# A weight unit's high-part products ahead of its low-part products; norms, transposes and products by halves of 512 columns

## The chip, the cores and the metric

The kernel runs on one core of one Trainium2 chip. The metric is the device time of one execution in microseconds. TensorE is called PE here, VectorE is DVE, ScalarE is ACT, GpSimd is POOL, and SyncE, which issues the large loads, is SP.

## What is computed

One sequence of 256 tokens with 1024 features goes through two blocks, all in float32. The first block has two hybrid layers (a linear-recurrent mixer beside banded attention, then a squared-ReLU network of width 4096). The second has a pooling mixer with a gated network of width 2816, then a sparse-attention mixer and eight gated experts of width 3584, of which every token uses two. Cut to the parts that the change touches:

```python
def hybrid_layer(x, ...):                      # twice
    h = rms_norm(x, norm1_g)
    proj = h @ w_in
    ...
    x = x + jnp.concatenate([y_m, y_a], axis=-1) @ w_out
    u = jax.nn.relu(rms_norm(x, norm2_g) @ w_up)
    return x + (u * u) @ w_down

def second_block(x, ...):
    for i in range(DEPTH):                     # i = 0: pool and swiglu, i = 1: nsa and experts
        ...
        x = layer_norm(ALPHA * x + h, ln_g[i, 0], ln_b[i, 0])
        ...
        x = layer_norm(ALPHA * x + f, ln_g[i, 1], ln_b[i, 1])

def swiglu(x, w_gu, w_down):
    g, u = jnp.split(x @ w_gu, 2, axis=-1)
    return (jax.nn.silu(g) * u) @ w_down
```

## The kernel before

**Units.** All weights are laid out ahead of time as 491 units of up to 128 x 2048 numbers (1 MB). SP loads them in order into a ring of four slots, and of six in the experts (`slot`, `sync_program`); a slot is loaded anew once DVE has read it (`low.of(last)`). For each unit ACT rounds the weights to a shorter float format and writes `HI` (`split_hi`, L499), and then DVE writes the rest, weight minus `HI`, as `LO` (`split_lo`, L507). `HI` and `LO` have three buffers each, and ACT waits until PE has used unit u - 3 (`used`).

**Products.** Activations are split in the same way into `XTH` and `XTL` (of the rows, turned) or `HTH` and `HTL` (of a network's hidden values). A product is taken as high x high, high x low weight, and low activation x high weight, three matmuls for each block of 128 rows (`group3`, L517). An expert with up to 64 tokens is packed: its high and low activations stand side by side in 128 columns, and two matmuls do (`group2`, L527). PE takes all matmuls of a block of rows before it goes to the next block, so the second matmul of a unit already needs `LO`; it waits for `low.of(u)` ahead of the whole unit, in `col_part` (units by columns: projections, and "up" and "gate" of a network), in `row_part` ("down") and in `few` (units of 8 to 48 columns).

**Norms.** Two tiles of 128 tokens (t = 0 and 1) follow one another. `rms_apply` and `ln_apply` end with one DVE instruction over all 1024 columns (L740, L775) into `ROWS` or `X`. `turn_rows` waits for it (`rows_at`), turns the first four blocks of 128 columns into one bank (L693) and the other four into the next. ACT copies each bank to `XTH` (`cols_hi`, L701) and DVE writes the rest to `XTL` (`cols_lo`, L709). The products wait for the second bank (`x_ready`, the event "cols", t, 4). The functions put matmuls without use, on constants, where PE would stand still (`idle`, L675, and `idle_first`, L682).

**A network.** `net_tensor` goes over chunks c of 512 hidden columns: two units up, two units gate (where it is gated), then the turning of chunk c - 1 (`net_turn_tensor`, L1032; for a packed expert matmuls against `pairs`, L1027), then two units down of chunk c - 2. ACT and DVE take the units in the same order, two units ahead of PE. On ACT, `net_turn_scalar` for a packed expert holds in this order: the silu of the turned bank (L1042), one unit of `split_hi`, the copy to the high half of `HTH` (L1058), and the other units. On DVE, `net_turn_vector` holds the product with the gate (L1068), one unit of `split_lo`, the low half (L1084), and the other units. Each engine works strictly in its own order. In the execution shown, expert 0 has one full and one packed tile, experts 1 to 3 one full tile each, and experts 4 to 7, from about 1825 us on, one packed tile each.

Of the kernel before, what the change touches and what calls it, by code (L numbers as in the profile page):

```python
# [16 lines left out]
P = 128  # L17
# [348 lines left out]
def build(nc, d, out, tables):  # L366
    at, cons_cols, units, place = tables
    dense = len(units) - N_EXP * d["experts"].shape[1]
    with ExitStack() as ctx:
# [143 lines left out]
        def group3(e, out_ap, trios, start, stop):  # L513
            n, m = 0, 3 * len(trios)
            for lh, ll, rh, rl in trios:
                for a, b in ((lh, rh), (lh, rl), (ll, rh)):
                    ins = e.matmul(out_ap, lhsT=a, rhs=b, start=start and n == 0,  # L517
                                   stop=stop and n == m - 1)
                    n += 1
            return ins  # L520

        def group2(e, out_ap, duos, start, stop):

            n, m = 0, 2 * len(duos)
            for both, rh, rl in duos:
                for b in (rh, rl):
                    ins = e.matmul(out_ap, lhsT=both, rhs=b, start=start and n == 0,  # L527
                                   stop=stop and n == m - 1)
                    n += 1
            return ins  # L530
# [6 lines left out]
        def col_part(e, use, t, u, i, last, kinds, a, x_ready):  # L537
# [4 lines left out]
            for w in x_ready(t):  # L542
                e.wait_ge(*w)
            e.wait_ge(*low.of(u))
            if kinds[t] == P:
                xh, xl = (XTH, XTL) if u < dense else (XM[:, 0], XM[:, 1])
                ins = group3(e, bank[:, 0:n], [
                    (xh[:, i * kk + k, a:a + P], xl[:, i * kk + k, a:a + P], hv[:, k, :], lv[:, k, :])
                    for k in range(kk)], i == 0, last)
            else:  # L550
                ins = group2(e, bank[:, 0:n], [
                    (XP[:, i * kk + k, 2 * a:2 * a + P], hv[:, k, :], lv[:, k, :])
                    for k in range(kk)], i == 0, last)
# [34 lines left out]
        def row_part(e, use, t, u, i, kb, hb, first, stop, kinds, h_ready):  # L588

            hv, lv = hi_lo(u)  # L590
            for w in h_ready:
                e.wait_ge(*w)
            e.wait_ge(*low.of(u))
            for nh in range(2):
                end = stop and 2 * i + 2 == kb
                if kinds[t] == P:
                    ins = group3(e, banks.get(*use, t, nh), [
                        (HTH[:, hb, 2 * i + k, tile(t)], HTL[:, hb, 2 * i + k, tile(t)],
# [33 lines left out]
        def x_ready(name):  # L632

            return lambda t: [v_bank.of(name, "cols", t, 4)]

        def few(e, use, key, x_ready):
# [5 lines left out]
            for t in range(2):  # L642
                for w in x_ready(t):
                    e.wait_ge(*w)
# [2171 lines left out]
```

## Time and profile before

| | |
|---|---|
| Median of three runs | 2314.14 us (2311.27 to 2316.27) |
| The profiled execution | 2311.63 us |
| Its span | 2309.8 us |
| Busy in the span | PE 2154.1 us, DVE 1595.7, ACT 1322.8 |
| Granted TensorE clock, mean | 0.977 |
| HBM read | 521.48 MB, 226 GB/s over the span |

The span is the time from the first to the last instruction; 1.8 us of the execution lie around it. The chain of waits is read from the last instruction back: at each step to what released it. A bracket behind a row of the timeline gives how long the engine had been idle and what ended that. PE's matmuls overlap, and a busy time counts each to its modelled end (0.39 us for 512 columns), so the pace of a stream is read from the distance between starts. The share of the DMA engines passes 1.00 by a little where they are full, since their packets overlap.

### The profile page before, as it was taken

What the parts mean: (1) busy time and instruction counts of PE and PEld (TensorE: products, weight loads), DVE (VectorE), ACT (ScalarE), POOL (GpSimd) and SP (SyncE); (2) the same over time, 40 slices, a digit from 0 to 9 for tenths busy, and PEclk for the clock granted to TensorE, in tenths of its full rate; (3) what the DMA queues carried; (4) which work ended last, traced back from release to release, by engine and by line L of the source; (5) the groups of instructions that cost most, each with busy time, mean ns of one, the idle gap of its engine ahead of it and who ended that gap; (6) DMA issues with size and microseconds to landing.
All of it is one profiled execution on the core that took longest, in us unless ns stands there. A gap on an engine that the chain in (4) does not pass through costs nothing.

```text
span 2309.8 us, 26107 instructions
## 1 busy us (share of the span) xinstructions
PE 2154.1 (93%) x10090; PEld 1723.0 (75%) x10090; DVE 1595.7 (69%) x1538; ACT 1322.8 (57%) x1376; POOL 22.1 (1%) x33
## 2 busy tenths in 40 slices
PE   8889999989999999998888999999999989898987
PEld 6667887767788788776667888788888776666665
DVE  4965555776555644565745554888888889898997
ACT  5554444644444444436534544676767778787886
POOL 0000000000000000000000000000000000000000
PEclk9989999999999999997899999999999999999999
DMA  6314553431655355441007555698888999999995
GB/s 259 137 46 150 182 182 129 165 119 69 243 186 186 137 183 195 150 148 59 1 19 281 199 214 194 255 373 344 346 346 338 373 348 415 350 411 352 411 369 216
DMA packets 74337, 524.29 MB, mean 227 GB/s; under 512 B 8704, under 2 KB 9152, under 8 KB 11872
## 3 DMA queue, kind: packets, MB, share of 16 engines
q1 hardware_dynamic: 71424, 511.64, 58.4%
q0 software_dynamic: 2784, 10.93, 1.3%
q8 instruction: 82, 1.34, 0.2%
q14 instruction: 47, 0.39, 0.0%
HBM read 521.48 MB, written 1.05 MB: 226 GB/s over the span
## 4 chain that ended last, share of the span: by engine, by line
PE 71%; DVE 16%; ACT 8%; issue 5%; DMA 0%; DVEq 0%; ACTq 0%; POOLq 0%
PE psum L517 51%; PE psum L527 8%; DVE LO L507 6%; ACT HI L499 3%; PE psum L1027 3%; DVE AR L1512 1%; PE psum L2362 1%; PE psum L1032 1%; PE psum L2390 1%; PE psum L881 1%; ACT AR L847 1%; DVE XT L709 1%; PE psum L693 1%; PE psum L675 1%; PE psum L818 1%
## 5 line engine op out<-in xcount | busy, mean ns | idle before, releaser
L507 DVE TENSOR_TENSOR LO<-ring,HI 128x2048 fp32r<-128x2048 f32 x379 | 851.4, 2259 | 415.4 <-ACT HI L499 409.2
L499 ACT ACTIVATE HI<-ring 128x2048 fp32r<-128x2048 f32 x379 | 713.0, 1886 | 339.9 <-PE psum L517 279.5
L517 PE MATMUL psum<-HI,XT 128*128 128x512 f32 (+1 forms) x2592 | 827.6, 394 | 34.9 <-DVE XT L709 12.1
L517 PEld LDWEIGHTS psum<-HI,XT 128*128 128x128 f32 x2592 | 493.7, 191 | 159.1 <-DVE XT L709 24.5
L517 PE MATMUL psum<-LO,XT 128*128 128x512 f32 (+1 forms) x1296 | 506.7, 391 | 0.0
L507 DVE TENSOR_TENSOR LO<-AR,HI 128x2048 fp32r<-128x2048 f32 x112 | 254.3, 2290 | 48.3 <-ACT HI L499 47.8
L517 PEld LDWEIGHTS psum<-LO,XT 128*128 128x128 f32 x1296 | 248.0, 191 | 48.5
L527 PE MATMUL psum<-HI,XT 128*128 128x512 f32 x560 | 231.1, 413 | 39.9 <-DVE LO L507 38.4
L499 ACT ACTIVATE HI<-AR 128x2048 fp32r<-128x2048 f32 x112 | 213.4, 1911 | 61.5 <-PE psum L527 37.4
L517 PE MATMUL psum<-HI,HTH 128*128 128x512 f32 x568 | 225.1, 396 | 0.0
L517 PE MATMUL psum<-HI,HTL 128*128 128x512 f32 x568 | 221.6, 390 | 0.0
L517 PE MATMUL psum<-LO,HTH 128*128 128x512 f32 x568 | 221.2, 389 | 0.0
L527 PE MATMUL psum<-LO,XT 128*128 128x512 f32 x560 | 220.4, 394 | 0.0
L527 PEld LDWEIGHTS psum<-HI,XT 128*128 128x128 f32 x560 | 105.5, 188 | 99.2 <-issue 40.7
L990 ACT ACTIVATE AR<-psum 128x512 f32<-128x512 f32 (+1 forms) x107 | 63.5, 594 | 111.1 <-PE psum L517 92.0
L517 PEld LDWEIGHTS psum<-HI,HTL 128*128 128x128 f32 x568 | 106.6, 188 | 22.7
L517 PEld LDWEIGHTS psum<-LO,HTH 128*128 128x128 f32 x568 | 106.8, 188 | 21.1
L517 PEld LDWEIGHTS psum<-HI,HTH 128*128 128x128 f32 x568 | 106.7, 188 | 20.8
L527 PEld LDWEIGHTS psum<-LO,XT 128*128 128x128 f32 x560 | 105.8, 189 | 20.6 <-issue 1.0
L527 PE MATMUL psum<-HI,HTH 128*128 128x512 f32 x280 | 112.6, 402 | 5.0 <-DVE HTH L1084 4.6
L527 PE MATMUL psum<-LO,HTH 128*128 128x512 f32 x280 | 109.5, 391 | 0.0
L1048 ACT ACTIVATE HTH<-psum 128x512 fp32r<-128x512 f32 (+1 forms) x72 | 42.7, 593 | 57.4 <-PE psum L1032 52.8
(279 smaller groups left out, 1886.7 us busy)
## 6 DMA issues: line engine op xcount, KB each, us to landing
ring<-in_experts SPq DMA_DIRECT2D x224, 1024.0 KB, 6.8
ring<-in_dense SPq DMA_DIRECT2D x149, 1024.0 KB, 4.8
AR<-in_experts SPq DMA_DIRECT2D x112, 1024.0 KB, 6.7
bcs<-in_ln_g POOLq DMA_DIRECT2D x4, 512.0 KB, 4.3
bcs<-in_ln_b POOLq DMA_DIRECT2D x4, 512.0 KB, 5.1
bcs<-in_norm_g POOLq DMA_DIRECT2D x3, 512.0 KB, 4.0
cons<-in_cons POOLq DMA_DIRECT2D x1, 1317.0 KB, 8.1
X<-in_x SPq DMA_DIRECT2D x2, 512.0 KB, 4.2
```

The source lines that it names most:

```text
L499: e.activation(HI[:, h:h + m], slot(u), ACT.Copy).then_inc(*high.up(u))
L507: e.tensor_tensor(LO[:, h:h + m], slot(u), HI[:, h:h + m].bitcast(F32), ALU.subtract).then_inc(*low.up(u))
L517: ins = e.matmul(out_ap, lhsT=a, rhs=b, start=start and n == 0, stop=stop and n == m - 1)
L527: ins = e.matmul(out_ap, lhsT=both, rhs=b, start=start and n == 0, stop=stop and n == m - 1)
L675: e.matmul(bank, lhsT=ident, rhs=cons[:, 0:512], start=True, stop=True)
L693: ins = e.transpose(bank[:, j * P:(j + 1) * P], src(k0 + j), ident)
L709: e.tensor_tensor(XTL[:, k0:k0 + 4, tile(t)], banks.get(name, "cols", t, k0).rearrange("p (k s) -> p k s", k=4), XTH[:, k0:k0 + 4, tile(t) ...
L818: e.matmul(bank[:, 0:2 * nk], lhsT=a.qT[:, b, tile(qt)], rhs=a.kz(kind, b)[:, :, 0:nk], start=True, stop=True).then_inc(*filled.up(a.name, ...
L847: e.activation(w3[:, h, :], w3[:, h, :], ACT.Exp, bias=nm[:, h:h + 1], accum_out=l[:, 2 * b + h:2 * b + h + 1]).then_inc(*a_done.up(a.name ...
L990: e.activation(GS[:, hb, t, 0:n], banks.get(use, "up", c, t)[:, 0:n], f).then_inc(*a_bank.up(use, "up", c, t))
L1027: ins = e.matmul(bank[:, o:o + PACK], lhsT=src[:, tile(j)], rhs=C("pairs"), start=True, stop=True)
L1048: e.activation(HTH[:, hb, 0:nb, tile(t)], bank[:, 0:n].rearrange("p (j s) -> p j s", j=nb), ACT.Copy).then_inc(*a_done.up(use, "turn", c, t))
```

## The change

1. `products` takes the place of `group3` and `group2`. For a unit, PE waits for `high.of(u)` and does all matmuls on `HI` (8 in a full tile, 4 in a packed one); then it waits for `low.of(u)` and does those on `LO` (4). Their number is the same. In `row_part` the high-part matmuls of both halves stand ahead of the low-part ones of both.
2. `x_ready` takes the block that is needed: a unit of blocks 0 to 3 waits for the first turned bank alone.
3. `rms_apply` and `ln_apply` end with two instructions over 512 columns each, and `turn_rows` waits for each half by itself. Where the rows come from the mixers (`y_tile`), each half waits for its own event.
4. The output goes out in four DMAs of 512 columns in place of two of 1024.

```diff
+        def products(e, out_ap, pairs, start, stop):
+
+            for n, (a, b) in enumerate(pairs):
+                ins = e.matmul(out_ap, lhsT=a, rhs=b, start=start and n == 0,
+                               stop=stop and n == len(pairs) - 1)
             return ins
...
-            for w in x_ready(t):
+            for w in x_ready(t, kk * (i + 1) - 1):
                 e.wait_ge(*w)
+            if kinds[t] == P:
+                xh, xl = [z[:, i * kk:i * kk + kk, a:a + P] for z in
+                          ((XTH, XTL) if u < dense else (XM[:, 0], XM[:, 1]))]
+                first = [(z[:, k], hv[:, k, :]) for k in range(kk) for z in (xh, xl)]
+            else:
+                xh = XP[:, i * kk:i * kk + kk, 2 * a:2 * a + P]
+                first = [(xh[:, k], hv[:, k, :]) for k in range(kk)]
+            e.wait_ge(*high.of(u))
+            products(e, bank[:, 0:n], first, i == 0, False)
             e.wait_ge(*low.of(u))
...
+            ins = products(e, bank[:, 0:n], [(xh[:, k], lv[:, k, :]) for k in range(kk)], False, last)
...
+            e.wait_ge(*high.of(u))
+            for nh in range(2):
+                products(e, banks.get(*use, t, nh), [
+                    (z[:, hb, 2 * i + k, tile(t)], hv[:, k, half(nh)]) for k in range(2)
+                    for z in ((HTH, HTL) if kinds[t] == P else (HTH,))], first and i == 0, False)
             e.wait_ge(*low.of(u))
...
-            return lambda t: [v_bank.of(name, "cols", t, 4)]
+            return lambda t, k: [v_bank.of(name, "cols", t, k // 4 * 4)]
...
-                for w in ready:
+                for w in ready(k0 // 4):
                     e.wait_ge(*w)
...
-            e.scalar_tensor_tensor(dst[:, t, :], X[:, t, :], r, gv, ALU.mult,
-                                   ALU.mult).then_inc(*v_done.up(name, "rows", t))
+            for nh in range(2):
+                e.wait_ge(*g_at)
+                e.wait_ge(*v_order.last)
+                e.scalar_tensor_tensor(dst[:, t, half(nh)], X[:, t, half(nh)], r, gv[:, half(nh)],
+                                       ALU.mult, ALU.mult).then_inc(*v_done.up(name, "rows", t, nh))
+            v_done.mark(name, "rows", t)
...
             for t in range(2):
-                e.wait_ge(*v_done.of("l3", "rows", t))
-                e.dma_start(out[0, tile(t), :], X[:, t, :]).then_inc(s_out, 16)
-            e.wait_ge(s_out, 32)
+                for nh in range(2):
+                    e.wait_ge(*v_done.of("l3", "rows", t, nh))
+                    e.dma_start(out[0, tile(t), half(nh)], X[:, t, half(nh)]).then_inc(s_out, 16)
+            e.wait_ge(s_out, 64)
```

PE before, in a chunk of the last packed expert: the end of the second unit "gate", and the turning behind it (`HI` and `LO` are the weight's parts, `XT` the activations; a wait stands with the instruction that it holds up).

```order
L527 MATMUL psum<-HI,XT 128x512 [waits s_low]
L527 MATMUL psum<-LO,XT 128x512
L527 MATMUL psum<-HI,XT 128x512
L527 MATMUL psum<-LO,XT 128x512
L527 MATMUL psum<-HI,XT 128x512
L527 MATMUL psum<-LO,XT 128x512
L527 MATMUL psum<-HI,XT 128x512
L527 MATMUL psum<-LO,XT 128x512
L1027 MATMUL psum<-cons,AR 128x64 [waits s_a_bank]
L1027 MATMUL psum<-cons,AR 128x64 x7
```

PE now, in the same place:

```order
L516 MATMUL psum<-HI,XT 128x512 [waits s_high]
L516 MATMUL psum<-HI,XT 128x512 x3
L516 MATMUL psum<-LO,XT 128x512 [waits s_low]
L516 MATMUL psum<-LO,XT 128x512 x3
L1025 MATMUL psum<-cons,AR 128x64 [waits s_a_bank]
L1025 MATMUL psum<-cons,AR 128x64 x7
```

The wait for DVE has moved from ahead of eight matmuls to ahead of the last four, and one wait, for ACT, has come in ahead of the first.

DVE before, at the program's start: the norm of tile 0, its columns' low part, the norm of tile 1, and the low parts of the first two units.

```order
L740 SCALAR_TENSOR_TENSOR AR<-X,SML,bcs 128x1024 [waits s_v_done,s_first]
L709 TENSOR_TENSOR XT<-psum,XT 128x4x128 [waits s_v_done,s_a_done]
L709 TENSOR_TENSOR XT<-psum,XT 128x4x128 [waits s_v_bank,s_a_done]
L733 TENSOR_TENSOR SML<-SML 128x1 [waits s_v_bank,s_a_done]
L737 RECIPROCAL SML<-SML 128x1 [waits s_v_done,s_a_done]
L740 SCALAR_TENSOR_TENSOR AR<-X,SML,bcs 128x1024 [waits s_v_done]
L507 TENSOR_TENSOR LO<-ring,HI 128x2048 [waits s_high] x2
```

DVE now, in the same place:

```order
L731 SCALAR_TENSOR_TENSOR AR<-X,SML,bcs 128x512 [waits s_v_done,s_first]
L731 SCALAR_TENSOR_TENSOR AR<-X,SML,bcs 128x512 [waits s_v_done]
L699 TENSOR_TENSOR XT<-psum,XT 128x4x128 [waits s_v_done,s_a_done]
L699 TENSOR_TENSOR XT<-psum,XT 128x4x128 [waits s_v_bank,s_a_done]
L723 TENSOR_TENSOR SML<-SML 128x1 [waits s_v_bank,s_a_done]
L727 RECIPROCAL SML<-SML 128x1 [waits s_v_done,s_a_done]
L731 SCALAR_TENSOR_TENSOR AR<-X,SML,bcs 128x512 [waits s_v_done] x2
L507 TENSOR_TENSOR LO<-ring,HI 128x2048 [waits s_high] x2
```

Each norm's last instruction has become two of half its columns; nothing else on DVE has changed its place, and ACT's order is the same as before.

## Rows read from the trace of the kernel before

**Rows 1.** Chain of waits, whole program; start us, us, engine, line, instructions

```profile
by line: PE psum L517 51.4%; PE psum L527 8.3%; DVE LO L507 6.2%; issue 5.0%; ACT HI L499 3.3%; PE psum L1027 2.6%; DVE AR L1512 1.4%; PE psum L2362 1.3%; PE psum L1032 1.3%; PE psum L2390 1.0%; PE psum L881 0.9%; ACT AR L847 0.7%; DVE XT L
...
365.39 21.79 PE psum L517 x96
```

**Rows 2.** Who waited for whom, 1850 to 2250 us; us, times, longest

```profile
PE psum L527 <- DVE LO L507: 34.7, 53, 1.9
DVE LO L507 <- ACT HI L499: 30.9, 42, 1.4
```

**Rows 3.** Stretches; PE, PEld, DVE, ACT, POOL busy, clock, DMA share, GB/s

```profile
1650.00:1700.00 50.00, 50.00 (x227) 41.36 (x226) 44.14 (x25) 36.23 (x24) 0.00 (x0) 1.00 0.94 366
...
1904.40:1919.80 15.40, 13.86 (x66) 10.50 (x65) 14.06 (x8) 12.87 (x11) 0.00 (x0) 1.00 1.01 420
...
1850.00:2250.00 400.00, 360.16 (x1695) 273.62 (x1696) 356.97 (x225) 319.72 (x261) 0.00 (x0) 1.00 0.96 379
```

**Rows 4.** Timeline, one chunk of a packed expert; start us, us, engine, line

```profile
1893.77 4.49 DVE L507 TENSOR_TENSOR LO<-AR,HI 128x2048 fp32r<-128x2048 f32 x2
...
1898.31 0.50 PE L527 MATMUL psum<-HI,XT 128*128 128x512 f32 x1
...
1898.49 4.49 DVE L507 TENSOR_TENSOR LO<-ring,HI 128x2048 fp32r<-128x2048 f32 x2 [0.24 <-ACT HI L499]
...
1900.26 1.89 PE L1027 MATMUL psum<-cons,AR 128*128 128x64 f32 x16
...
1902.19 0.38 ACT L1042 ACTIVATE AR<-psum 128x256 f32<-128x256 f32 x1 [1.13 <-PE psum L1027]
...
1902.47 1.91 ACT L499 ACTIVATE HI<-ring 128x2048 fp32r<-128x2048 f32 x1
...
1902.90 0.41 DVE L1068 TENSOR_TENSOR AR<-AR,psum 128x256 f32<-128x256 f32 x1
...
1904.41 2.29 DVE L507 TENSOR_TENSOR LO<-ring,HI 128x2048 fp32r<-128x2048 f32 x1 [1.10 <-ACT HI L499]
...
1906.62 0.42 DVE L1084 TENSOR_TENSOR HTH<-AR,HTH 128x256 fp32r<-128x256 f32 x1
```

**Rows 5.** Timeline, second norm of layer 0

```profile
196.69 1.03 PE L693 MATMUL psum<-cons,AR 128*128 128x128 f32 x8
...
197.56 1.02 PE L675 MATMUL psum<-cons 128*128 128x512 f32 x2
197.96 1.49 DVE L709 TENSOR_TENSOR XT<-psum,XT 128x512 fp32r<-128x512 f32 x2 [2.93 <-ACT XT L701]
...
199.50 0.50 PE L517 MATMUL psum<-HI,XT 128*128 128x512 f32 x1 [0.91 <-DVE XT L709]
...
202.79 0.50 PE L517 MATMUL psum<-HI,XT 128*128 128x512 f32 x1 [0.27 <-DVE LO L507]
...
205.67 1.28 DVE L740 SCALAR_TENSOR_TENSOR AR<-X,SML,bcs 128x1024 f32<-128x1024 f32 x1
...
207.01 1.09 PE L693 MATMUL psum<-cons,AR 128*128 128x128 f32 x8 [0.35 <-DVE AR L740]
...
209.88 0.50 PE L517 MATMUL psum<-HI,XT 128*128 128x512 f32 x1 [0.91 <-DVE XT L709]
```

**Rows 6.** Timeline, the program's start

```profile
14.42 3.69 ACT L499 ACTIVATE HI<-ring 128x2048 fp32r<-128x2048 f32 x2
...
16.35 4.49 DVE L507 TENSOR_TENSOR LO<-ring,HI 128x2048 fp32r<-128x2048 f32 x2 [0.32 <-ACT HI L499]
...
18.79 0.47 PE L517 MATMUL psum<-HI,XT 128*128 128x512 f32 x1 [3.23 <-DVE LO L507]
...
24.32 1.03 PE L693 MATMUL psum<-cons,AR 128*128 128x128 f32 x8
```

**Rows 7.** Timeline, the norm ahead of the router

```profile
1199.31 1.97 PE L693 MATMUL psum<-cons,X 128*128 128x128 f32 x8 [3.21 <-DVE X L775]
...
1202.74 0.67 PE L517 MATMUL psum<-XT,HI 128*8 128x256 f32 x2
```

More of the change, by code:

```diff
@@ L595, in row_part @@
                 end = stop and 2 * i + 2 == kb
-                if kinds[t] == P:
-                    ins = group3(e, banks.get(*use, t, nh), [
-                        (HTH[:, hb, 2 * i + k, tile(t)], HTL[:, hb, 2 * i + k, tile(t)],
-                         hv[:, k, half(nh)], lv[:, k, half(nh)]) for k in range(2)],
-                        first and i == 0, end)
-                else:
-                    ins = group2(e, banks.get(*use, t, nh), [
-                        (HTH[:, hb, 2 * i + k, tile(t)], hv[:, k, half(nh)], lv[:, k, half(nh)])
-                        for k in range(2)],
-                        first and i == 0, end)
+                ins = products(e, banks.get(*use, t, nh), [
+                    (HTH[:, hb, 2 * i + k, tile(t)], lv[:, k, half(nh)]) for k in range(2)], False, end)
                 if (t, nh) == (len(kinds) - 1, 1):
@@ L642, in few @@
             for t in range(2):
-                for w in x_ready(t):
+                for w in x_ready(t, KB - 1):
                     e.wait_ge(*w)
+            e.wait_ge(*high.of(u))
+            products(e, bank[0:n, 0:S], [(hv[:, i, :], z[:, i, :]) for i in range(KB)
+                                         for z in (XTH, XTL)], True, False)
             e.wait_ge(*low.of(u))
-            ins = group3(e, bank[0:n, 0:S], [
-                (hv[:, i, :], lv[:, i, :], XTH[:, i, :], XTL[:, i, :]) for i in range(KB)], True, True)
+            ins = products(e, bank[0:n, 0:S], [(lv[:, i, :], XTH[:, i, :]) for i in range(KB)],
+                           False, True)
             ins.then_inc(*used.up(u))
@@ L1317, in second_rows @@
             def second_rows():
-                turn_rows(e, n1, 1, lambda k: ROWS[:, 1, tile(k)], rows_at(n1, 1), wait=l, rest=l, b=BA[0])
+                turn_rows(e, n1, 1, lambda k: ROWS[:, 1, tile(k)], rows_of(n1, 1), wait=l, rest=l, b=BA[0])
                 if l == 0:
@@ L1773, in pool_tensor @@
             idle(e, 3)
-            turn_rows(e, "l0", 0, lambda k: X[:, 0, tile(k)], [v_done.of("l0", "rows", 0)], rest=0)
+            turn_rows(e, "l0", 0, lambda k: X[:, 0, tile(k)], rows_of("l0", 0), rest=0)
             mixed_tensor(e, 1)
@@ L1950, in sparse_tensor @@
             xr = x_ready("l1")
-            turn_rows(e, "l1", 0, lambda k: X[:, 0, tile(k)], [v_done.of("l1", "rows", 0)])
+            turn_rows(e, "l1", 0, lambda k: X[:, 0, tile(k)], rows_of("l1", 0))
             cols_by_tile(e, ("q0", 2), ("q0", 2), BOTH, xr, between=lambda: turn_rows(
-                e, "l1", 1, lambda k: X[:, 1, tile(k)], [v_done.of("l1", "rows", 1)], wait=1, b=BA[0]))
+                e, "l1", 1, lambda k: X[:, 1, tile(k)], rows_of("l1", 1), wait=1, b=BA[0]))
             cols(e, ("q1", 2), ("q1", 2), BOTH, xr)
@@ L2419, in experts_tensor @@
         def experts_tensor(e):
-            turn_rows(e, "l2", 0, lambda k: X[:, 0, tile(k)], [v_done.of("l2", "rows", 0)])
-            turn_rows(e, "l2", 1, lambda k: X[:, 1, tile(k)], [v_done.of("l2", "rows", 1)], wait=4)
+            turn_rows(e, "l2", 0, lambda k: X[:, 0, tile(k)], rows_of("l2", 0))
+            turn_rows(e, "l2", 1, lambda k: X[:, 1, tile(k)], rows_of("l2", 1), wait=4)
             few(e, ("gates", 3), ("gates", 3), x_ready("l2"))
```

58 lines of the change are left out of this document (17 added, 41 removed).

## Prediction

> **What bounds the kernel now.** I read the chain of waits first. 51% of it is matmuls at L517, the full tiles; 8% is L527, the packed tiles; 6% is DVE's `LO` and 3% ACT's `HI`. A run of 96 matmuls over four units takes 21.79 us, 0.227 us each, with no pause at any unit's start [rows 1]. There PE is the bound, and an order that adds and removes no matmul gives nothing. In 1650 to 1700 us, experts with a full tile, PE is busy for all 50 us [rows 3].
>
> So the gain has to come from two other kinds of place. One is experts 4 to 7, the last 470 us. In 1850 to 2250 us PE waits 34.7 us for `LO`, 53 times, and DVE waits 30.9 us for `HI`, 42 times [rows 2]. DVE is busy 357.0 of these 400 us, and the DMA engines are at a share of 0.96 [rows 3]: three resources stand near their limit. The other kind is the norms, where PE stands still while DVE, PE, ACT and DVE hand one tile on [rows 5 to 7].
>
> **Packed experts: the cycle.** Rows 4 is one chunk, and the pattern comes back every 15.40 us: the `LO` of "down" at 1898.49 is that of the next chunk at 1913.9. The reader is to follow it round. DVE ends the `LO` of the second gate unit at 1893.77 + 4.49 = 1898.26. PE starts that unit's 8 matmuls at 1898.31 and turns at 1900.26: 1.95 us. Turning takes until 1902.15, the silu starts at 1902.19, and only behind it, at 1902.47, does ACT take the `HI` of the next chunk's first unit. DVE gets it for its `LO` at 1904.41, after 1.10 us of idling. Then come four `LO`, 2.2 us apart, and the small L1084 (1906.62, a step of 0.34), and the ring closes at 1913.66. The two `LO` of "down" (1898.49, 4.49 us) run beside PE's and ACT's part.
>
> Now the four matmuls on `HI` can run before 1898.26, since that `HI` was ready before DVE read it. Four of eight remain behind `LO`: 1.95 - 4 x 0.23 = 1.03 us. Turning, silu, `HI` and the next `LO` come 0.92 us earlier, and the cycle becomes 15.40 - 0.92 = 14.48 us. DVE is next: it is busy 14.06 of 15.40 us in a chunk [rows 3], so 1.34 us of idling (1.10 and 0.24) are there, and 0.92 fits. PE has slack: 48 x 0.23 + 1.89 = 12.9 us. From 1825 us to the end there are some 28 such cycles with those that hold an expert's change: 28 x 0.92 = 26 us, and 0.9 at the very end, where four matmuls run ahead of the last `LO`. That is 27 us if nothing else stands in the way.
>
> **Packed experts: the loads.** A chunk reads six units, 6 x 1.049 = 6.29 MB. In the chunk of 1904.4 to 1919.8 us the DMA share is 1.01 at 420 GB/s [rows 3]. At that pace six units take 6.29 / 0.420 = 15.0 us, more than the 14.48 that the cycle asks for. Over the 400 us the share is 0.96 at 379 GB/s: there are stretches at a full share and a lower rate, so not every packet moves at the best pace, and I take the share and not the best rate as the measure. What DMA could still give is 1 - 0.96 / 1.01 = 5%, 20 us in 400. It can't all be had: at an expert's change DVE does other work, the six slots are full and the queue pauses, whatever the pace elsewhere. I take four fifths, 16 us, in place of 27. Ends for the range: 27 (loads never bind), and 2 (loads give nothing, but four matmuls at the very end and slack in the ring remain). 16 is nearer to the row of 0.96.
>
> The Trainium skill (DMA: Bandwidth & Descriptors, "Where 436 GB/s comes from") says that for loads from HBM the HBM side binds at about 358 GB/s, and names 435 GB/s as the ceiling of the ports. By the first, an estimate, a chunk would take 6.29 / 0.358 = 17.6 us, which the trace contradicts with 15.40 [rows 3, 4]. By the second it would take 14.46 us, the loads would not bind, and the sum would be the 27 us of the second rival; the row with a share of 1.01 at 420 speaks against it.
>
> **Start** [rows 6]. PE waits 3.23 us for the first `LO` (ended 18.65). The `HI` of that unit ends at 16.3. Its 8 matmuls then run to 18.2, the 4 others from 18.7 to 19.6, and the second unit (8 matmuls, then 4, its `LO` ready by 20.8) to 22.4. Tile 1 is turned then and not at 24.32: 1.9 us. Behind it PE needs only the first turned bank, 0.8 us earlier (below). Together 2.7 us.
>
> **Norms, tile 0** [rows 5]. PE turns at 196.69, fills with a useless matmul until 198.6, and waits for both banks of L709 (197.96 + 1.49 = 199.45). With the first bank alone (half of the 1.49) it goes on at 198.7: 0.8 us. At 202.79 it waits for the `LO` of the second unit, 0.27 us and a slow restart; this goes too. But the gain of tile 0 is not kept by itself: tile 1's norm stands behind that `LO` on DVE, which doesn't move.
>
> **Norms, tile 1** [rows 5]. The norm's last step runs 205.67 to 206.95, and PE, which by then waits, turns at 207.01. Two instructions over 512 columns take 1.49 us at L709, about 0.75 each, where the one over 1024 takes 1.28. So the first half is there at 206.4, and the second at 207.16, 0.2 us later than before. PE turns four blocks, then four more, fills until 208.5, and goes on at 208.55 in place of 209.88. So 1.3 us for the norm. The 0.2 us are paid on DVE at each norm, and they are hidden behind PE's first four blocks; where nobody uses the halves (the norm ahead of pooling), they show.
>
> The same pattern stands at three norms of the hybrid layers (3 x 1.3 = 4.0), at the one after pooling (1.1, less the 0.2 of the norm ahead of it) and ahead of the sparse layer (1.8, since there tile 0's norm is late as well). At the two mixer outputs both tiles gain (2 x 1.4), at the sparse one tile 1 alone (0.8). Ahead of the router the second half of the turning runs at the lower clock, and both tiles' norms are on the path: 1.3 of the 3.4 us from 1199.31 to 1202.74 [rows 7]. The first expert and the output give 0.7. Sum: 2.7 + 4.0 + 1.1 + 1.8 + 2.8 + 0.8 + 1.3 + 0.7 = 15.2 us. What follows each place (mixers, DVE's chains) is moved as a whole; the loads of the dense units are far ahead there. Bounds: 9 (only tile 1's half turns up) to 19.
>
> **Sum.** 15 + 16 = 31 us off the profiled 2311.6: 2280.6. The median of the runs lies 2.5 above the profiled one, so 2283.
>
> **Rivals.** *Loads don't bind.* The packed experts run at 14.48 us per chunk: 15 + 27 = 42 us off, 2272. For it: no wait for a landing in any view. Against: a share of 1.01.
>
> *Loads give nothing more.* The stretches of low rate at a full share are how the engines behave when asked for more; then only the norms and the end stay: 15 + 2 = 17 off, 2297. For it: 1.01 in a chunk of 15.40 us. Against: 0.96 in the mean.
>
> *Slower: each new wait costs a restart.* PE gets one more wait in each of 491 units. Where a wait really holds PE up, the next matmul starts late: the step from the first to the second is 0.34 us and not 0.23 (from 24 matmuls in 5.53 us at the start, 18.79 to 24.32 [rows 6], one sees 0.23). If an unneeded wait in the middle of a group cost the same 0.11 us, 491 x 0.11 = 54 us would stand against 31: 2314 + 23 = 2337. It turns to slower from 31 / 491 = 0.063 us for a wait. Against it: the 96 matmuls of rows 1 pass four such satisfied waits at 0.227 us each; 0.063 us would be seen.
>
> *It doesn't do what it says* would be PE still waiting for `LO` as long as before; then some 5 us from the norms' halves, within what can't be told apart.
>
> **Chances.** Loads bind in part, 2283: 0.58. Loads don't bind, 2272: 0.16. Loads give nothing more, 2297: 0.19. Within 0.2% (about what a measurement of this kernel can tell from no change): 0.03. Slower: 0.04. So faster 0.93. The range goes from the bound of the second case, with 19 for the norms (2314 - 46 = 2268), to that of the third with 11 to 13 (2300).
>
> **What would show it.** In the profile after: PE's wait for `LO` at the start at most 0.5 us; PE's start of the second unit's matmuls at 22.4 us less the tile's turn; the three norms' resumption 1.3 us earlier against their turn. In the packed experts a chunk of 14.8 to 15.0 us, a DMA share of 1.00 or more in all stretches from 1850 us on, and, new, ACT's `HI` waiting for landings; the wait of DVE for `HI` in other chunks below 0.3 us. A chunk of 14.5 us is the first rival, one of 15.3 the second. In full tiles 0.227 us for a matmul; anything above shows the slower rival. Wrong would be the whole sum if PE, with its matmuls earlier, met the bank evictions of ACT as a new wait at each chunk.

## The result and the profile after

The changed kernel takes 2275.97 us in the median (2274.03 to 2279.28). The ratio to the kernel before is 0.984, with an interval of 0.9823 to 0.9857. The profiled execution takes 2274.03 us where that of before took 2311.63: 37.6 us less. Forecast were 31 us less and a median of 2283 us, in a range of 2268 to 2300. Sign and size came out; the way there partly did not.

The waits in 1850 to 2250 us, for [rows 2]. The columns are us in total, times, longest.

```profile
PE psum L516 <- DVE LO L507: 12.4, 21, 2.0
...
DVE LO L507 <- ACT HI L499: 17.6, 26, 1.4
...
ACT HI L499 <- DMA AR<-in_experts: 1.5, 3, 0.6
...
ACT HI L499 <- DMA ring<-in_experts: 0.6, 2, 0.4
```

Each of the first two was over 30 us. The last two are new and small: ScalarE waits for a landing, five times. All products now stand at L516.

The stretches, for [rows 3] (busy of PE, PEld, DVE, ACT, POOL; clock, DMA share, GB/s):

```profile
1650.00:1700.00 50.00, 50.00 (x224) 41.24 (x223) 43.21 (x24) 37.05 (x25) 0.00 (x0) 1.00 0.98 372
1850.00:2250.00 400.00, 375.29 (x1773) 285.89 (x1772) 373.98 (x237) 334.70 (x274) 0.00 (x0) 1.00 0.97 396
1889.00:1904.40 15.40, 14.36 (x67) 10.80 (x67) 14.88 (x10) 13.63 (x11) 0.00 (x0) 1.00 1.01 419
```

PE and DVE are 15 and 17 us busier in the same 400 us, and the loads bring 396 GB/s in place of 379. One chunk, for [rows 4]:

```profile
1880.51 1.89 PE L1025 MATMUL psum<-cons,AR 128*128 128x64 f32 x16
...
1882.44 0.39 ACT L1040 ACTIVATE AR<-psum 128x256 f32<-128x256 f32 x1 [1.13 <-PE psum L1025]
1882.72 1.91 ACT L499 ACTIVATE HI<-ring 128x2048 fp32r<-128x2048 f32 x1
...
1884.67 2.29 DVE L507 TENSOR_TENSOR LO<-ring,HI 128x2048 fp32r<-128x2048 f32 x1 [0.51 <-ACT HI L499]
...
1893.82 4.49 DVE L507 TENSOR_TENSOR LO<-ring,HI 128x2048 fp32r<-128x2048 f32 x2
...
1895.01 1.89 PE L1025 MATMUL psum<-cons,AR 128*128 128x64 f32 x16
...
1896.94 0.39 ACT L1040 ACTIVATE AR<-psum 128x256 f32<-128x256 f32 x1 [1.13 <-PE psum L1025]
```

Turning starts at 1880.51 and again at 1895.01, the silu at 1882.44 and 1896.94: a chunk is 14.50 us and was 15.40. (The four middle steps of the first three packed experts are 14.47 to 14.53 us, and were 15.39 to 15.45; most are 14.48.) DVE idles 0.51 us for the `HI` behind the silu, not 1.10, and the idling of 0.24 ahead of the two `LO` of "down" is gone. That is the ring of the prediction, shorter by 0.92 us to within what one reads.

Where the 37.6 us went I read from the ends of `LO` of the same weight units in both traces. Up to the 330th unit (about 1850 us) the changed kernel is 16.7 us ahead. From there to the last unit it takes 419.7 us and not 440.1, 20.4 less. The 330th is the seventh unit of expert 4; from that expert's first unit to it both traces take 18.5 us, so all that the packed experts gain lies behind it. The tail gives 0.4.

### The profile page after: what moved, and what is told of

It reads as the page before. It is cut to its first block, busy times and chain, and to the rows that moved or that the text cites. A ratio compares the mean times of both kernels' runs of the same rounds, so it can differ in the third digit from the quotient of the medians.

```text
span 2272.2 us, 26134 instructions
## 1 busy us (share of the span) xinstructions
PE 2151.1 (95%) x10090; PEld 1724.3 (76%) x10090; DVE 1597.7 (70%) x1556; ACT 1320.2 (58%) x1376; POOL 22.1 (1%) x33
## 3 DMA queue, kind: packets, MB, share of 16 engines
q8 instruction: 82, 1.34, 0.2%
## 4 chain that ended last, share of the span: by engine, by line
PE 70%; DVE 18%; ACT 6%; issue 5%; DMA 0%; DVEq 0%; ACTq 0%; SPq 0%; POOLq 0%
PE psum L516 58%; DVE LO L507 10%; ACT HI L499 3%; PE psum L1025 2%; DVE AR L1508 1%; PE psum L1030 1%; PE psum L2358 1%; PE psum L816 1%; PE psum L879 1%; PE psum L1895 1%; PE psum L664 1%; PE psum L683 1%; ACT AR L845 1%; PE psum L2386 1%; PE psum L1272 1%
## 5 line engine op out<-in xcount | busy, mean ns | idle before, releaser
L516 PE MATMUL psum<-HI,XT 128*128 128x512 f32 (+1 forms) x3152 | 805.1, 394 | 21.0 <-issue 5.8
L516 PEld LDWEIGHTS psum<-HI,XT 128*128 128x128 f32 x3152 | 592.2, 191 | 164.0 <-issue 13.1
L516 PE MATMUL psum<-LO,XT 128*128 128x512 f32 (+1 forms) x1856 | 507.5, 395 | 18.6 <-DVE LO L507 14.4
L516 PEld LDWEIGHTS psum<-LO,XT 128*128 128x128 f32 x1856 | 342.7, 190 | 123.0 <-DVE LO L507 56.6
L516 PE MATMUL psum<-HI,HTH 128*128 128x512 f32 x848 | 303.3, 398 | 4.9 <-DVE HTH L1082 4.9
L516 PE MATMUL psum<-LO,HTH 128*128 128x512 f32 x848 | 227.2, 390 | 0.0
L516 PE MATMUL psum<-HI,HTL 128*128 128x512 f32 x568 | 221.5, 390 | 0.0
L516 PEld LDWEIGHTS psum<-HI,HTH 128*128 128x128 f32 x848 | 157.3, 188 | 37.0 <-DVE HTH L1082 6.5
L516 PEld LDWEIGHTS psum<-LO,HTH 128*128 128x128 f32 x848 | 159.2, 188 | 33.9
L516 PEld LDWEIGHTS psum<-HI,HTL 128*128 128x128 f32 x568 | 106.8, 188 | 21.0
L845 ACT ACTIVATE AR<-AR,SML 128x256 f32<-128x256 f32 (+1 forms) x96 | 45.4, 473 | 44.7 <-DVE SML L837 40.8
L1025 PEld LDWEIGHTS psum<-cons,AR 128*128 128x128 f32 x560 | 66.8, 192 | 3.0 <-ACT AR L996 1.2
L1025 PE MATMUL psum<-cons,AR 128*128 128x64 f32 x560 | 66.6, 272 | 1.0 <-ACT AR L996 1.0
L1072 DVE TENSOR_TENSOR HTL<-psum,HTH 128x512 fp32r<-128x512 f32 (+1 forms) x72 | 49.3, 684 | 22.5 <-ACT HTH L1046 16.9
L816 PE MATMUL psum<-AR 128*128 128x512 f32 (+1 forms) x96 | 54.0, 656 | 11.2 <-DVE AR L833 7.0
L691 ACT ACTIVATE XT<-psum 128x512 fp32r<-128x512 f32 x40 | 23.9, 597 | 64.4 <-PE psum L683 63.4
```

The lines of the kernel that those rows point to most:

```text
L691: e.activation(XTH[:, k0:k0 + 4, tile(t)], banks.get(name, "cols", t, k0).rearrange("p (k s) -> p k s", k=4), ACT.Copy).then_inc(*a_done.u ...
L816: e.matmul(bank[:, 0:2 * nk], lhsT=a.qT[:, b, tile(qt)], rhs=a.kz(kind, b)[:, :, 0:nk], start=True, stop=True).then_inc(*filled.up(a.name, ...
L845: e.activation(w3[:, h, :], w3[:, h, :], ACT.Exp, bias=nm[:, h:h + 1], accum_out=l[:, 2 * b + h:2 * b + h + 1]).then_inc(*a_done.up(a.name ...
L1025: ins = e.matmul(bank[:, o:o + PACK], lhsT=src[:, tile(j)], rhs=C("pairs"), start=True, stop=True)
L1072: e.tensor_tensor(HTL[:, hb, 0:nb, tile(t)], bank[:, 0:n].rearrange("p (j s) -> p j s", j=nb), xh.bitcast(F32), ALU.subtract).then_inc(*v_ ...
```

## The experiments

Two columns recur below. "Ahead" is the time to the end of `LO` of the 330th unit, "packed" that from there to the last unit's.

| kernel | median us | ratio to before (95%) | ahead | packed |
|---|---|---|---|---|
| before | 2312.4 to 2314.1 | 1 | 1849.9 | 440.1 |
| after | 2276.0 | 0.984 (0.9823 to 0.9857) | 1833.2 | 419.7 |
| products_only | 2289.2 | 0.9889 (0.9864 to 0.9913) | 1852.3 | 419.9 |
| halves_only | 2300.6 | 0.9942 (0.9924 to 0.9959) | 1839.2 | 439.8 |
| one_unit | 2307.3 | 0.9974 (0.9961 to 0.9988) | 1846.2 | 434.0 |
| two_units | 2296.0 | 0.9927 (0.9910 to 0.9943) | 1850.5 | 423.3 |
| more_waits | 2276.5 | 0.9847 (0.9831 to 0.9864) | 1835.1 | 419.9 |
| light_loads | 2277.5 | 0.985 (0.9834 to 0.9867) | 1838.0 | 419.6 |
| hi_early | 2271.4 | 0.9831 (0.9808 to 0.9853) | 1832.3 | 416.1 |
| hi_early_light | 2262.3 | 0.9786 (0.9770 to 0.9803) | 1833.7 | 407.6 |
| fill | 2275.1 | 0.9827 (0.9804 to 0.985) | 1837.6 | 420.9 |
| after_again | 2274.8 | 0.984 (0.9822 to 0.9857) | 1833.5 | 419.8 |

### Each part alone

products_only takes the halves out of the changed kernel: the norms' last step, the waits ahead of turning, the waits for turned columns and the output transfer are whole again.

```diff
-            for nh in range(2):
-                e.scalar_tensor_tensor(dst[:, t, half(nh)], X[:, t, half(nh)], r, gv[:, half(nh)], ...
+            e.scalar_tensor_tensor(dst[:, t, :], X[:, t, :], r, gv, ALU.mult, ...
...
-            return lambda t, k: [v_bank.of(name, "cols", t, k // 4 * 4)]
+            return lambda t, k: [v_bank.of(name, "cols", t, 4)]
```

> The changed kernel with its norms, transposes, waits for turned columns and output transfer whole again (1024 columns), so that only the order of the products is new. Theory (the two parts are independent and add up): the chunk of the packed experts stays at 14.48 us, 20.4 us are gained from 1815 us on, 2 at the start (the first LO wait) and 1 in small restarts: 2288 us, a ratio of 0.990 to the kernel before, that is 13 us above the changed kernel. Rival (the halves are needed for the order to pay, or the other way round): under 5 us between this kernel and the changed one.

halves_only keeps these and restores the old order of products. Here is `col_part`, the branch taken alone; `row_part` and `few` are changed in the same way:

```diff
-            e.wait_ge(*high.of(u))
-            products(e, bank[:, 0:n], first, i == 0, False)
             e.wait_ge(*low.of(u))
-            ins = products(e, bank[:, 0:n], [(xh[:, k], lv[:, k, :]) for k in range(kk)], False, last)
+            ins = products(e, bank[:, 0:n], [
+                q for k in range(kk) for q in ([first[m * k], second[k]] + first[m * k + 1:m * k + m])],
+                i == 0, last)
```

> The changed kernel with the products in the order of the kernel before (high, low, high of each block, one wait for LO), norms, transposes and waits by halves kept. Theory (parts add up): the chunk is back at 15.40 us, the three norms of the hybrid layers keep 1.3 us each, in sum 13 to 14 us from the norms and transposes: 2298 us, ratio 0.994. Rival (part of the 16.7 us before the packed experts is not from the halves but from where TensorE's granted clock happens to fall): the sum comes out between 8 and 20 us, and the difference from 14 stands in stretches in which the clock is at 1.2 GHz in one kernel and at 2.4 in the other.

The packed experts get all of their gain from the order (419.9 against 419.7) and none from the halves (439.8 against 440.1). Ahead of them it is the other way round. A stretch in which the clock stays at 2.4 GHz in all of them shows it best: from the 21st to the 56th unit, the whole first feed-forward with a norm at either end. First before, then after:

```profile
202.74:410.91 208.17, 202.95 (x921) 164.80 (x922) 112.47 (x96) 92.77 (x90) 0.54 (x1) 1.00 0.47 168
```

```profile
194.14:399.65 205.51, 201.31 (x917) 163.74 (x916) 113.23 (x99) 92.77 (x90) 0.54 (x1) 1.00 0.48 171
```

Then halves_only and products_only:

```profile
200.56:406.22 205.66, 202.60 (x921) 164.85 (x922) 113.12 (x99) 92.77 (x90) 0.54 (x1) 1.00 0.48 171
```

```profile
199.33:407.49 208.16, 202.12 (x921) 164.44 (x920) 112.56 (x97) 92.74 (x90) 0.54 (x1) 1.00 0.48 168
```

2.7 us for two norms with both parts, 2.5 with the halves alone, 0.0 with the order alone. The sum of the parts' medians, 23.2 and 11.8 us, is 35.0, within a few us of the whole (36.9): the parts add up as closely as these medians can tell.

### Which wait closes the ring

one_unit is the kernel before with the new order in one of a chunk's six units, two_units in both gate units:

```diff
+            if kinds[t] == PACK and len(kinds) == 1 and use[1] == "gate" and last:
+                e.wait_ge(*high.of(u))
+                products(e, bank[:, 0:n], first, i == 0, False)
+                e.wait_ge(*low.of(u))
+                ins = products(e, bank[:, 0:n], second, False, last)
```

(two_units leaves out `and last`.)

> The kernel before (order, norms and transposes), with the new order of products in a single place: the second gate unit of each chunk in the experts whose only tile is packed. Theory (the ring of waits runs through that unit alone): the chunk is 14.48 us as in the changed kernel, the gain is the 20 us of the packed experts, 2291 us, ratio 0.991. Rival (each unit's wait for LO takes part): one of six units changed gives about a sixth, 3 to 4 us, 2308 us, chunk 15.3.

My theory fell here. The ring does pass through this unit, as the prediction followed it, but a chunk takes 15.09 us and 6.1 us are gained in all, not 20. (A spell of low clock from 1972.4 us, of 3.4 us, hides some 1.6 more: the expert that it falls in takes 115.2 us, the one before it 113.6. It doesn't save the theory.) The timeline of PE in one_unit:

```profile
1891.53 0.47 PE L516 MATMUL psum<-HI,XT 128*128 128x512 f32 x1 [0.18 <-DVE LO L507]
...
1893.45 1.07 PE L516 MATMUL psum<-HI,XT 128*128 128x512 f32 x4
1894.35 1.08 PE L516 MATMUL psum<-LO,XT 128*128 128x512 f32 x4
1895.27 1.89 PE L1035 MATMUL psum<-cons,AR 128*128 128x64 f32 x16
...
1910.36 1.89 PE L1035 MATMUL psum<-cons,AR 128*128 128x64 f32 x16
```

PE starts the first gate unit behind its `LO`, at 1891.53, and then has 16 matmuls in a row. It gets to the second unit's four on `HI` at 1893.45 only, and to the four on `LO` at 1894.35, although DVE wrote that `LO` by 1893.6. The bound has moved one unit back: from the end of the first gate unit's `LO` to turning it takes 1895.27 - 1891.39 = 3.88 us, and took 1900.26 - 1896.06 = 4.20 [rows 4]. That is the 0.31 us of the chunk.

> The kernel before, with the new order of products in both gate units of each chunk in the experts whose only tile is packed. With the second gate unit alone the chunk was 15.08 us, not 14.48: TensorE, which ran all 8 matmuls of the first gate unit behind that unit's LO, had 16 matmuls in a row (16 x 0.23 = 3.7 us) from there, and they ended 0.33 us earlier than before and no more. Theory: with both gate units changed, four matmuls of each are ahead of their LO, TensorE waits for the second LO again, and the chunk is 14.48 us: the gain is the 20 us of the packed experts, 2291 us, ratio 0.991. Rival (the up and down units count as well): the chunk comes out between 14.6 and 15.0 us, 2296 to 2303 us.

16.8 of the 20.4 us. The chunk:

```profile
1916.97 2.29 DVE L507 TENSOR_TENSOR LO<-ring,HI 128x2048 fp32r<-128x2048 f32 x1 [0.33 <-ACT HI L499]
...
1931.63 2.29 DVE L507 TENSOR_TENSOR LO<-ring,HI 128x2048 fp32r<-128x2048 f32 x1 [0.34 <-ACT HI L499]
```

14.66 us, 0.18 above the 14.48 of most chunks of the full change. The four other units of a chunk bring that rest; that it is the up units, which still run all behind their `LO` and so push PE a little late into the gate units, is my reading, and no run takes them by themselves. So of the 0.92 us the last gate unit alone brings 0.31, the unit ahead of it 0.43, the rest 0.18. Here a wait at the end of a run of units was left behind only as far as PE had caught up before it.

### The price of a wait

```diff
             for n, (a, b) in enumerate(pairs):
+                if probe:
+                    e.e.wait_ge(*probe)
                 ins = e.matmul(out_ap, lhsT=a, rhs=b, ...
```

> The changed kernel with a wait (always satisfied: the same HI that the unit's first matmul waited for) ahead of each of the 8 matmuls on HI of the up and gate units with a full tile in the experts, some 780 waits more. Theory (a satisfied wait costs nothing): 2276 us, 0.227 us for a matmul. Rival (each costs the restart of 0.11 us): 86 us more, 2362 us; the point at which the whole change would have turned slower, 0.063 us, would show as 49 us more, 2325 us.

From the 198th to the 330th unit (the experts with one full tile, and the first units of the next) it is 409.4 us with the added waits and 409.2 without. PE in 1600 to 1650 us, where each matmul on `HI` of an up or gate unit has its wait:

```profile
1600.00:1650.00 50.00, 50.00 (x240) 42.05 (x239) 42.38 (x26) 34.92 (x24) 0.00 (x0) 1.00 0.88 341
```

240 matmuls start there, and 238 in the changed kernel. The slower rival is out: at the 0.063 us where it would have decided, 49 us would be missing.

### Do the loads bind?

light_loads halves every load from the fifth expert on; the other half of each slot keeps old weights, so the products there are of old numbers while the engines' work stays the same. hi_early has full loads and a quicker ring: ScalarE's `HI` goes ahead of the silu, so that DVE needn't wait for it. hi_early_light has both.

```diff
+                dst = slot(u)
+                if u >= dense and x >= 4:
+                    dst, src = dst[:, 0:UNIT // 2], src[:, 0:UNIT // 2]
-                e.dma_start(slot(u), src).then_inc(s_ring[i], 16)
+                e.dma_start(dst, src).then_inc(s_ring[i], 16)
```

```diff
+            alone = tuple(kinds) == (PACK,)
+            if alone:
+                between()
             for t, kind in enumerate(kinds):
...
-            between()
+            if not alone:
+                between()
```

> The changed kernel, with each load of the packed experts (from the fifth expert on) fetching half of its unit, so that the products there use old weights in the other half; the engines' work is the same in number and size. Theory (the loads are at the edge in the changed kernel but hold it up for only some 2 us, as its waits of ScalarE for landings show): 2270 to 2274 us, chunk still 14.48 us. Rival (the loads are what is left of the bound there): the packed experts speed up by 8 us or more, to 2267 us or less, with a chunk below 14.4.

> The changed kernel, with ScalarE's HI of the next chunk's first unit in front of the silu and not behind it, in the experts whose only tile is packed. Theory (VectorE's wait for this HI, 0.51 us in a chunk, is the last slack of the ring, and the loads still have some: 42 units landing every 2.49 us are 104.6 us of an expert's 110.3): the chunk is 13.97 us, 22 x 0.5 = 11 us less than the changed kernel, 2265 us, ratio 0.980; ScalarE's waits for landings grow by some us. Rival (the loads bind at 14.5 us already): the chunk stays at 14.4 to 14.5, 2274 to 2278 us, and what VectorE no longer waits for HI, ScalarE waits for landings, some 10 us more.

> The kernel with ScalarE's HI ahead of the silu, with half-size loads as in the other one. Theory (with full loads it stayed at 2271 because six landings of 2.49 us are 14.94 us, more than its 13.97): without that bound the chunk is 13.97 us, 22 x 0.5 = 11 us less than with half loads alone, 2260 to 2262 us. Rival (VectorE or TensorE bounds it at the same time, not the loads): within 3 us of the other kernel with half loads.

In the changed kernel the loads cost nothing that can be read: half the bytes, DMA share 0.60 in place of 0.97, and the packed experts take 419.6 us in place of 419.7.

```profile
1850.00:2250.00 400.00, 376.45 (x1784) 286.24 (x1782) 374.22 (x237) 333.13 (x272) 0.00 (x0) 1.00 0.60 200
```

(The median of light_loads is 1.5 us above that of the changed kernel; its trace is 4.8 us later at the 330th unit, and all but the last few loads up to there are whole. More on that below.)

With the quicker ring they do. hi_early gains 3.6 us in the packed experts where the ring allows 12.1 (407.6 with half loads, my 11 and a little). Who waits for landings in hi_early, 1850 to 2250 us, and one piece of ScalarE:

```profile
ACT HI L499 <- DMA ring<-in_experts: 8.3, 14, 1.6
...
ACT HI L499 <- DMA AR<-in_experts: 4.5, 9, 0.6
```

```profile
1900.98 1.92 ACT L499 ACTIVATE HI<-AR 128x2048 fp32r<-128x2048 f32 x1 [0.58 <-DMA AR<-in_experts]
...
1903.47 1.92 ACT L499 ACTIVATE HI<-ring 128x2048 fp32r<-128x2048 f32 x1
1905.96 1.91 ACT L499 ACTIVATE HI<-ring 128x2048 fp32r<-128x2048 f32 x1 [0.57 <-DMA ring<-in_experts]
...
1908.45 1.92 ACT L499 ACTIVATE HI<-ring 128x2048 fp32r<-128x2048 f32 x1
```

From 1900.98 on a `HI` starts each 2.49 us, 0.02 us behind its landing, and six landings there (1900.95 to 1915.89) are 14.94 us. PE follows some units behind. Within the expert it still turns every 13.88 us; the time is lost where the next expert begins:

```profile
1892.49 1.89 PE L1025 MATMUL psum<-cons,AR 128*128 128x64 f32 x16
...
1906.36 1.89 PE L1025 MATMUL psum<-cons,AR 128*128 128x64 f32 x16
1911.83 1.89 PE L1025 MATMUL psum<-cons,AR 128*128 128x64 f32 x16
...
1945.90 1.90 PE L1025 MATMUL psum<-cons,AR 128*128 128x64 f32 x16
```

The last step is 34.07 us; in hi_early_light it is 31.25 (1913.15 to 1944.40). At the next two changes of expert 1.9 and 2.1 us are lost in the same way, 6.8 of the 8.5 us in all. So the chunk of my theory came, 13.88 us for 13.97, and the gain didn't; the rival's chunk of 14.4 to 14.5 didn't come, and its waits for landings did (8.3 + 4.5 us). I had set the landings against the mean of an expert alone, 104.6 us against 110.3; even the 107.2 that an expert takes in hi_early_light leave room for them, and still the loads bind. hi_early is the quickest kernel with whole loads, but its interval (0.9808 to 0.9853) overlaps that of the changed kernel, so I don't call it better.

### TensorE's clock ahead of the packed experts

The order changes nothing at the norms, and yet products_only is 2.4 us *later* than before at the 330th unit, while one_unit, which but for the last few units is the kernel before up to there, is 3.7 us earlier. They part most from the 141st to the 157th unit: before takes 229.2 us there, with 57.9 us at 1.2 GHz, products_only 232.7 with 69.3, one_unit 225.9 with 44.7. A shorter stretch, from the 16th to the 21st unit (the end of the first mixer), shows it closer. Before, after and hi_early (the same instructions as after up to the packed experts):

```profile
123.84:202.74 78.90, 69.39 (x345) 52.88 (x343) 48.73 (x84) 38.03 (x74) 0.53 (x1) 0.94 0.21 74
```

```profile
120.57:194.14 73.57, 66.06 (x348) 50.36 (x347) 48.96 (x85) 37.31 (x73) 0.53 (x1) 0.98 0.22 79
```

```profile
121.31:198.90 77.59, 70.24 (x351) 54.13 (x350) 48.96 (x85) 38.03 (x74) 0.54 (x1) 0.93 0.21 75
```

The clock falls to 1.2 GHz for some us and comes back. In before that is so for 10.2 us of the stretch, in after for 3.4, in hi_early for 10.2. At the same low time, before against hi_early, the change brings 1.3 us here. light_loads, with 10.2 us of low clock as well, but at other instructions, takes 75.7 us, 3.2 less than before. So of after's 5.3 us, 1.3 to 3.2 are the change's (forecast 1.4), and the rest is a spell of low clock that did not fall in this stretch. The norm behind pooling is the reverse. Before, after, hi_early:

```profile
597.68:796.10 198.42, 194.08 (x911) 160.14 (x910) 110.87 (x105) 88.98 (x89) 1.57 (x3) 1.00 0.47 169
```

```profile
583.37:782.33 198.96, 195.88 (x911) 161.40 (x910) 111.84 (x109) 88.98 (x89) 1.58 (x3) 0.99 0.48 170
```

```profile
587.18:784.47 197.29, 194.22 (x911) 160.19 (x910) 111.86 (x109) 88.99 (x89) 1.58 (x3) 1.00 0.49 171
```

1.1 us gained at full clock (forecast 1.1), and 0.5 lost where a low spell of 3.4 us fell in. So I asked what brings the spells, with three useless matmuls at each of three waits in the sparse layer, ahead of the longest spell:

```diff
+                if (kind, t) != (0, 0):
+                    idle(e, 3, BA[0])
                 bank = banks.take(e, "KZ", kind, t)
```

> The kernel with ScalarE's HI ahead of the silu, and three useless matmuls (0.43 us each) ahead of each of three groups of transposes of the sparse layer's keys, where TensorE waits 0.9, 1.5 and 1.2 us for a bank. In every kernel so far TensorE is granted 1.2 GHz for 17 to 20 us from there on, right behind these waits. Theory (the low spell follows the idling there): the spell of 20 us is gone or much shorter, the stretch gets up to 10 us shorter for 0.3 us more of matmuls, 2262 to 2268 us. Rival (the idling of these waits isn't what brings the low clock there): the spell stays where it is, 2270 to 2273 us.

PE in hi_early and, with the matmuls, in fill:

```profile
1040.00:1045.00 5.00, 4.78 (x21) 4.35 (x21) 3.86 (x9) 3.85 (x6) 0.00 (x0) 0.50 0.01 3
1045.00:1050.00 5.00, 5.00 (x22) 4.64 (x21) 2.42 (x2) 2.52 (x5) 0.00 (x0) 0.50 0.00 0
```

```profile
1040.00:1045.00 5.00, 5.00 (x16) 2.28 (x15) 3.31 (x7) 0.99 (x2) 0.00 (x0) 1.00 0.00 0
1045.00:1050.00 5.00, 5.00 (x40) 4.63 (x38) 2.52 (x7) 4.16 (x8) 0.00 (x0) 1.00 0.00 0
```

The spell of 20.5 us from 1038.7 is gone. A shift of the spells doesn't explain that: light_loads has the eight spells ahead of this place at the same times as fill, to 0.3 us, and has 20.5 us of low clock from 1040.8. So the spell did follow the idling. But nothing is won: at the doubled clock PE runs into waits (it is busy 3.39 of the 5 us from 1050 and 1.97 of those from 1055), the clock falls at 1054.3 for 10.2 us and again at 1067.9 for 17.1, and from the 141st to the 151st unit fill takes 84.7 us where hi_early took 84.3 and light_loads 84.7. There the clock is not what bounds the work. fill's median lies 3.7 us above hi_early's and its profile 10.0: 5.2 up to the 330th unit, where light_loads with the same early spells is as late (1838.0), and 4.8 in the packed experts, where the code is the same and the loads set the pace. But the profiled execution is the slowest of fill's four (2270.3, 2271.0, 2279.3, 2279.6), and hi_early's four (2269.6 to 2271.6, and 2278.9) lie in the same two places. So the two kernels aren't told apart, and what made the loads slower in this execution stays open.

> The changed kernel once more, for which spells of low clock repeat and which don't. Theory (the spell of 17 to 20 us in the sparse layer is in each run; the shorter ones fall differently from run to run in the same instructions): 2273 to 2279 us, the stretches before the packed experts differ by up to 3 us from the first profile wherever their low-clock time differs, and by under 0.3 us elsewhere; the packed experts take 419.7 us again. Rival (what differs between kernels is fixed by their instructions): all spells at the same instructions as in the first profile.

For this pair the rival was right. The second trace of the changed kernel has each of its 16 spells at the same instructions, to within 0.3 us: 20.5 us from 1036.1 and from 1036.3, 3.4 from 759.6 and from 759.8. hi_early_light, 0.3 us later at the 6th unit, has them too. But hi_early, light_loads, more_waits and fill, which share the first 1000 us of instructions with it, have some of them elsewhere, and they were 0.6 to 1.2 us later at the 6th unit. So in these traces the same spells go with the same course of the program, down to some tenths of a us, and with a small shift ahead they fall elsewhere. The instructions alone don't fix them, though, as the rival has it: the four runs of products_only have mean clocks of 0.973 to 0.981 and take 2283.3 to 2293.5 us. The spells' share of the 37.6 us can't be put at one number. The three traces of before's instructions reach the 330th unit at 1846.2 to 1850.5 us (mean 1848.9), the seven of after's (two of them with the added waits or matmuls) at 1832.3 to 1838.0 (mean 1834.8): the change is worth about 14 us there, and the single pair of profiles shows 16.7.

## Why the prediction was right, and where it wasn't

**The bound, full tiles.** Right. 96 matmuls still take 21.79 us [rows 1], and from the 198th to the 330th unit 409.2 us stand against 409.6.

**The cycle.** Right in mechanism and price: 14.48 us for most chunks, 0.92 less. DVE is the next to bound it: with the `HI` early and half loads it waits no more within an expert, and the chunk is 13.88. (Its wait for `HI` is 0.51 us and not below 0.3, since the 0.24 ahead of "down" went as well.) What the working left out is that PE must have caught up by the second gate unit; it had, since the change gives each unit its new order, and one_unit and two_units show what it would have cost otherwise.

**The number of cycles.** Mis-sized. I took 28 x 0.92 = 26 us, those that hold an expert's change among them. An expert takes 110.4 us and took 115.5: 5.2 us, what 5.6 cycles give and not 7. Of the seven steps from one turning to the next, in the first three packed experts, four are 0.92 shorter, the first 0.27, the short one at the end 0.0, and the one over the expert's change 1.26. There the ring runs another way: DVE idles 1.4 us for `HI` twice, before and after alike. The term is 20.4 us, and the very end gave 0.4 where I had 0.9.

**The loads.** This step failed. I set 6.29 / 0.420 = 15.0 us against the chunk's 14.48, as if each chunk had to live on its own six landings, and cut 27 to 16. light_loads shows that the cut was nothing: 0.1 us. An expert's 42 units need 42 x 2.49 = 104.6 us, and it takes 110.4; while DVE and PE do the work of an expert's change, the six slots fill, a landed unit waits up to 9.0 us for its `HI`, and the quick chunks behind it spend that lead at 14.94 - 14.48 = 0.46 us each. The lead just lasts: from unit to unit the wait of a landed unit falls to 0.02 us, and ScalarE waits for landings 2.1 us in all.

The mean is not the whole rule, and hi_early shows it. Its expert takes 108.8 to 110.0 us, though the engines need 107.2 (with half loads) and the landings 104.6. There each quick chunk spends 14.94 - 13.88 = 1.06 us of the lead, and the lead ends. It is not laid up again in full: around an expert's change some landings are 3 to 5 us apart, part of them issued late because the slots were full, part though issued long before (why stays open), so that the last three experts' first to last landings take 105.7 to 107.6 us and not 41 x 2.49 = 102.1. As I read these two kernels, what the slots hold when the quick chunks begin has to last through them. No run varies the number of slots.

The signs that I had named for this case stayed away: a chunk of 14.8 to 15.0 us, a share of 1.00 throughout (it was 0.97), and a `HI` waiting for landings but for those 2.1 us. So it was my case "loads don't bind", with 0.16, that described the machine. Its 27 us were 6 too many by the miscounted cycles and the end (20.4 + 0.4 were measured), and my 16 were 11 below it by the loads. Two errors of opposite sign left this term off by 4.8; that the total came so near is luck in that part. DMA is close all the same: hi_early was 0.6 us a chunk quicker in its ring, and there the loads took back 8.5 of 12.1 us.

**The loads, by the page.** hi_early's six landings are 6.29 MB in 14.94 us, 421 GB/s, at a share of 1.01. The Trainium skill (DMA: Bandwidth & Descriptors, "Where 436 GB/s comes from") has the HBM side bind at about 358 GB/s, a figure that it works out as half of what a stack gives its two cores. One core runs here, and the trace doesn't bear out 358 as its limit: the changed kernel takes in 396 GB/s over 400 us. The 435 GB/s that it names for the ports are above what was seen.

**Start.** 2.7 forecast. products_only is 1.6 us ahead at the 6th unit, halves_only 0.9, the changed kernel 3.7 in the first profile, 2.5 to 3.5 in the others. Turning of tile 1 starts at 21.47 against the forecast 22.4 ([rows 6]: 24.32):

```profile
15.45 2.08 PE L516 MATMUL psum<-HI,XT 128*128 128x512 f32 x8 [0.90 <-ACT HI L499]
17.69 1.20 PE L516 MATMUL psum<-LO,XT 128*128 128x512 f32 x4 [0.16 <-DVE LO L507]
...
21.47 1.03 PE L683 MATMUL psum<-cons,AR 128*128 128x128 f32 x8
```

The wait for `LO` is 0.16 us and was 3.23. What I missed is that the halves also start the first turning, and so ScalarE's first `HI`, a us earlier (13.41, [rows 6]: 14.42).

**Norms.** 1.3 us each was right (2.7 for two, at full clock). The norm's turn and resumption, for [rows 5]:

```profile
197.87 1.44 PE L683 MATMUL psum<-cons,AR 128*128 128x128 f32 x8 [1.18 <-DVE AR L731]
...
199.94 2.11 PE L516 MATMUL psum<-HI,XT 128*128 128x512 f32 x8
```

2.07 us from turn to resumption, where it was 2.87; the rest of the 1.3 is that the turn starts 0.81 us behind the start of the norm's last step (197.06) and not 1.34. Pooling gave the 1.1 of the forecast, the first mixer's output 1.3 to 3.2 for 1.4, once the clock is about the same. All places together gave about 14 us by the means of the traces, for a forecast of 15.2 less the output's part. What each of the sparse layer's places and the router's gave can't be told apart: from the 141st to the 157th unit TensorE is at 1.2 GHz for 45 to 64 us, and the stretch takes 225.9 to 229.2 us in three traces of before's instructions and 224.4 to 227.4 in three of after's.

**Slower.** Out: for a satisfied wait no price can be read (0.1 us over some 780 of them).

## What to carry to other kernels

Behind a ring of buffers, don't set a transfer's pace against the quickest chunk. Set it against the mean of the whole pattern (here an expert), and then ask whether the lead in the slots covers what the quick chunks spend of it: here it did at 0.46 us a chunk and didn't at 1.06. Count the steps of a pattern in the trace, each with its own gain, rather than dividing a span by one. Where a wait is to be left behind, check that the waiting engine gets there early enough: the run of work ahead of it sets that. Before a difference of a few us in a stretch is put down to an edit, compare the granted clock of the two, best with a second kernel whose instructions are the same there.

## What the hardware showed that I had not expected

- Some 780 further waits on an already reached semaphore, one for each matmul, cost nothing that can be read (409.4 against 409.2 us, 0.227 us for a matmul).
- The spells at 1.2 GHz came back at the same instructions in a second profiled execution, to 0.3 us, and some fell elsewhere where the program ran 0.6 us later. Other executions of one kernel differ in their mean clock (0.973 to 0.981 in products_only).
- The longest of them, 20.5 us, could be removed by 9 useless matmuls, and the time of its stretch stayed the same (84.7 us, and 84.3 and 84.7 in two traces with it): in that stretch the low clock cost nothing, since PE was not the bound.
- Loads of 1.049 MB land each 2.49 us, up to 31 in a row in the changed kernel, mostly with two or three others under way: 421 GB/s on one core, beside a DVE and a PE that are busy over 90% of the time.
